# Conditioning's sums in 32 by 32 squares on VectorE, and an embedding gate that begins with the first tile of tokens

## What is computed

```
# first block, from its second half on
hn = rms_norm(h, g_ffn_pre)
f_gate, f_up = split(hn @ w_ffn_in)              # 1024 -> 2 x 2816
f = (silu(f_gate) * f_up) @ w_ffn_out
h = h + rms_norm(f, g_ffn_post)
h = h + sigmoid(h @ w_ple_gate) * (p @ w_ple)    # the embedding's gate

# second block
cond = silu(c)                                   # 1024 values
mod = cond @ w_ada + b_ada                       # 1024 -> 6144
shift_mix, scale_mix, gate_mix, shift_ffn, scale_ffn, gate_ffn = split(mod)
h = rmsnorm(x, g_mix) * (1 + scale_mix) + shift_mix
qkv = h @ w_in                                   # then two kinds of attention,
                                                 # w_out, routing to 2 of 32 experts
```

## Time and profile before

| | us |
|---|---|
| median of 3 runs | 1155.83 |
| lowest and highest | 1154.67, 1155.89 |
| the profiled execution | 1153.45 |
| its span, first to last instruction | 1151.6 |
| TensorE busy | 1045.0 (91%) |
| VectorE busy | 492.2 (43%) |
| ScalarE busy | 377.3 (33%) |
| GpSimd busy | 493.2 (43%) |

### The profile page before, as it was taken

The page is one execution under the profiler, slowest core; times in us unless marked ns, Lnnn a source line. Parts: engine busy times, 40 slices in busy tenths (PEclk is TensorE's granted clock), DMA queues, the critical chain, the costliest instruction groups (busy, mean ns, idle before and its releaser), DMA issues.

```text
span 1151.6 us, 19857 instructions
## 1 busy us (share of the span) xinstructions
PE 1045.0 (91%) x8566; PEld 804.7 (70%) x8566; DVE 492.2 (43%) x886; ACT 377.3 (33%) x539; POOL 493.2 (43%) x209
## 2 busy tenths in 40 slices
PE   7999999998999999999999999898877788878676
PEld 6988999998799999888898895344433343424232
DVE  2999948467355465032245643222222121212112
ACT  6454544543654444444495432000000000000001
POOL 6895889875787888946465410000000000000000
PEclk9999999999999999999899999999999898989998
DMA  9554454356579989754233679999999999999994
GB/s 367 197 185 146 174 186 181 146 229 232 225 278 337 340 324 341 262 173 164 108 147 125 261 289 420 420 420 419 420 421 420 421 420 419 420 422 420 419 421 164
DMA packets 48330, 342.16 MB, mean 297 GB/s; under 512 B 5361, under 2 KB 5745, under 8 KB 7410
## 3 DMA queue, kind: packets, MB, share of 16 engines
q1 hardware_dynamic: 46944, 337.56, 74.3%
q10 hardware_dynamic: 1298, 3.32, 0.8%
HBM read 339.81 MB, written 1.05 MB: 296 GB/s over the span
## 4 chain that ended last, share of the span: by engine, by line
PE 60%; DMA 22%; DVE 11%; ACT 2%; SPq 2%; issue 1%; POOL 1%; DVEq 0%; ACTq 0%
DMA ring<-in_gu 17%; PE ps L469 14%; PE ps L471 14%; PE ps L470 14%; PE ps L1037 5%; DVE ps L1645 5%; DMA ar<-in_gu 5%; PE ps L1084 4%; PE ps L1073 2%; PE ps L1017 2%; SPq L2286 2%; PE ps L711 1%; POOL spl L2220 1%; DMA raw<-in_stream 1%; PE ps L462 1%
## 5 line engine op out<-in xcount | busy, mean ns | idle before, releaser
L2220 POOL TENSOR_TENSOR spl<-raw,sph 128x1024 fp32r<-128x1024 f32 x204 | 492.7, 2453 | 177.3 <-ACT sph L1139 177.2
L1139 ACT ACTIVATE sph<-raw 128x1024 fp32r<-128x1024 f32 x204 | 206.3, 1055 | 143.9 <-DMA raw<-in_stream 85.5
L469 PE MATMUL ps<-xbh,sph 128*128 128x256 f32 x608 | 173.5, 285 | 4.2 <-DVE xbl L1625 2.5
L470 PE MATMUL ps<-xbl,sph 128*128 128x256 f32 x608 | 172.7, 284 | 0.0
L471 PE MATMUL ps<-xbh,spl 128*128 128x256 f32 x608 | 172.7, 284 | 0.0
L469 PE MATMUL ps<-xah,sph 128*128 128x256 f32 x576 | 165.0, 286 | 1.1 <-DVE xal L1615 0.8
L470 PE MATMUL ps<-xal,sph 128*128 128x256 f32 x576 | 163.0, 283 | 0.0
L471 PE MATMUL ps<-xah,spl 128*128 128x256 f32 x576 | 162.9, 283 | 0.0
L2170 DVE TENSOR_TENSOR ar<-ar,ps 64x256 f32<-64x256 f32 x32 | 13.5, 423 | 275.4 <-ACT ar L1561 275.4
L1561 ACT ACTIVATE ar<-ps 64x256 f32<-64x256 f32 x32 | 12.1, 378 | 350.1 <-PE ps L1037 350.1
L1084 PE MATMUL ps<-ar,ar 128*128 128x512 f32 x256 | 125.7, 636 | 0.0
(11 more groups left out here) (292 smaller groups left out, 1337.3 us busy)
## 6 DMA issues: line engine op xcount, KB each, us to landing
raw<-in_stream SPq DMA_DIRECT2D x127, 1024.0 KB, 4.9
ring<-in_gu SPq DMA_DIRECT2D x116, 1024.0 KB, 27.0
ring<-in_dn SPq DMA_DIRECT2D x57, 1024.0 KB, 27.2
slotx<-in_gu SPq DMA_DIRECT2D x6, 1024.0 KB, 28.3
ar<-in_gu SPq DMA_DIRECT2D x6, 1024.0 KB, 26.3
ar<-in_dn SPq DMA_DIRECT2D x4, 1024.0 KB, 26.8
slotx<-in_dn SPq DMA_DIRECT2D x3, 1024.0 KB, 28.1
X<-in_x SPq DMA_DIRECT2D x2, 512.0 KB, 4.4
```

What stands on the lines that cost most here:

```text
L469: e.matmul(o, sh, mh, start=start, stop=False)
L470: e.matmul(o, sh, ml, start=False, stop=False)
L1139: e.activation(u.half(SPH[u.n % NSP], h), u.half(RAW[u.slot], h), ACTF.Copy).then_inc(w.up(hi_ok), 1)
L2220: e.tensor_tensor(u.half(SPLO[u.n % NSP], h), u.half(RAW[u.slot], h), u.half(SPH[u.n % NSP], h), ALU.subtract).then_inc(w.up(lo_ok), 1)
```

## The change

Five things change.

- Blocks of `w_ada` (the ten for the first 5120 columns): the last step stays in PSUM, and two instructions of VectorE follow every second unit. A transpose of each square of 32 by 32 brings 512 partial sums for each partition to `ADT`; a sum over 32 neighbours leaves 16 values in `ADS`. The sum over the partitions is then done but for its four groups of 32.
- `FOLD`, made once from the identity, adds these four groups up: four products of 32 by 40 on TensorE (L725 of the changed kernel) give all 40 columns of `MC` at once, between first-tile and second-tile work of the gate. The two `columns` are gone, and VectorE adds the bias for all 40 at once, ahead of the first gated quarter.
- X is turned a tile at a time, into two banks with one tile each: tile 0 ahead of w_ffn_out's last unit for tile 1, tile 1 behind the fold. ScalarE and VectorE copy tile by tile as well.
- The gate goes: unit 0 and 1 for tile 0; fold; tile 1 turned; unit 2 for tile 0; units 0, 1, 2 for tile 1; unit 3 for tile 0; unit 3 for tile 1. The quarters end in the order 0, 2, 1, 3 (`PARTS`), and sigmoids and gated sums follow it. On ScalarE the splits of later units now stand between the sigmoids in another way.
- Counts of semaphores follow. A slot of `RAW` is still free after the unit's four steps, not after the pair.

```diff
+        ADT = ADA[:, 4096:4608].rearrange("p (m c) -> p m c", m=16)
+        ADS = ADA[:, 4608:4768]
+        FOLD = ADA[:, 4768:4800]
...
             held.discard(ab)
-            free[ab] = [(ada_ok, 16)]
+            free[ab] = [(ada_ok, 20)]
             bb = token_major("w_out", XA, landed("merge", 1))
...
             for tt in ((0, 1), (0,), (1,)):
                 for c in range(8) if len(tt) == 2 else range(8, 11):
+                    if c == 10 and tt == (1,):
+                        turn_x2(0)
...
+                for s in range(4):
+                    mm = e.matmul(ps[b][32 * s:32 * s + 32, 0:40], FOLD, ADS.rearrange("p (j s) -> p s j", s=4)[:, s, :],
+                                  start=True, stop=True)
...
-            columns(0, 24)
+            part(0, 0, False, False)
+            part(1, 0, False, False)
+            held.clear()
+            held.update(gb)
+            turn_at[0] = bb[2]
+            columns()
             turn_x2(1)
-            bb = token_major("ple_gate", XB, landed("x2", 2))
+            part(2, 0, True, False)
+            part(0, 1, False, True)
+            part(1, 1, False, True)
+            part(2, 1, True, True)
+            part(3, 0, True, False)
+            part(3, 1, True, True)
...
             turn_old(0)
-            columns(24, 40)
...
                 if tt == 0:
                     take(wide_at[9])
                     take(wide_at[10])
+                    x2_high(0)
-            for n in range(4):
-                w.wait_ge(xt_mm, n + 1)
-                high(("x2", n), XB, 2 * n, None)
+            take(first["ple_gate"])
+            x2_high(1)
...
-            take(first["ple_gate"])
+            gate(0)
             take(first["ple_gate"] + 1)
-            gate(0)
-            gate(1)
             gate(2)
             take(first["ple_gate"] + 2)
+            gate(1)
             take(first["ple_gate"] + 3)
             gate(3)
...
+                if m % 2 and j < 10:
+                    own()
+                    e.transpose(ADT.rearrange("p m c -> p (m c)"), acc).then_inc(w.up(ada_ok), 1)
+                    own()
+                    e.tensor_reduce(ADS[:, 16 * j:16 * j + 16], ADT, AX, ALU.add).then_inc(w.up(ada_ok), 1)
...
+            e.tensor_reduce(FOLD, ident.rearrange("p (q r) -> p r q", q=4), AX, ALU.add).then_inc(w.up(az_ok), 1)
...
-                            w.wait_ge(ada_ok, 4 * ada_at.index(v - NRAW) + 4)
+                            w.wait_ge(ada_ok, ada_used[ada_at.index(v - NRAW)])
```

More of the change, by code:

```diff
@@ L682, in tensor, with turn_x2 @@
             held.update(bb)
+            def turn_x2(tt):
+                w.wait_ge(x_ok, X2 + 4 * tt + 4)
+                for half in range(2):
+                    b = bank(("x2", tt, half))
+                    claim(b)
+                    for k in range(4):
+                        o = (4 * half + k) * 128
+                        mm = e.transpose(ps[b][:, 128 * k:128 * k + 128], X[:, tt, o:o + 128], ident)
+                    mm.then_inc(w.up(xt_mm), 1)
+                    free[b] = [(act_lo, part_at["x2"] + 2 * tt + half + 1)]
             for tt in ((0, 1), (0,), (1,)):
                 for c in range(8) if len(tt) == 2 else range(8, 11):
+                    if c == 10 and tt == (1,):
+                        turn_x2(0)
                     w.wait_ge(ffm_ok, behind(c))
@@ L692, in tensor @@
             free[ab] = [(ada_ok, N_ADA)]
-            xb = [bank(("x2", n)) for n in range(4)]
-            def turn_x2(tt):
-                w.wait_ge(x_ok, X2 + 4 * tt + 4)
-                for k in range(8):
-                    o = (k % 2) * 256 + tt * 128
-                    claim(xb[k // 2])
-                    mm = e.transpose(ps[xb[k // 2]][:, o:o + 128], X[:, tt, k * 128:k * 128 + 128], ident)
-                    if tt and k % 2:
-                        mm.then_inc(w.up(xt_mm), 1)
@@ L713, in columns @@
                 mm.then_inc(w.up(mc_mm), 1)
-                free[b] = [(mc_ok, 2 if j0 else 1)]
-            turn_x2(0)
+                free[b] = [(mc_ok, 1)]
+            xb0 = [bank_of["x2", 0, half] for half in range(2)]
             held.clear()
-            held.update(xb)
+            held.update(xb0 + bb[2:])
             turn_at[0] = bb[0]
-            columns(0, 24)
-            turn_x2(1)
-            held.clear()
-            for n in range(4):
-                free[xb[n]] = [(act_lo, part_at["x2"] + 2 * n + 2)]
@@ L725, in tensor, with part @@
-            turn_at[0] = bb[0]
-            bb = token_major("ple_gate", XB, landed("x2", 2))
+            gb = [bank(("ple_gate", q)) for q in range(4)]
+            outs = [[ps[gb[2 * tt + j]][:, :] for tt in range(2)] for j in range(2)]
+            def part(n, tt, begun, done):
+                if n % 2 == 0:
+                    claim(gb[2 * tt + n // 2])
+                ready = None if begun else lambda k: (act_lo, part_at["x2"] + 2 * tt + k // 4 + 1)
+                tm_part("ple_gate", n, outs[n // 2], XB, ready, (tt,), done)
@@ L1878, in vector, with x2_low @@
                 m += 1
+            def x2_low(tt):
+                for half in range(2):
+                    c = slice(128 * tt, 128 * tt + 128)
+                    w.wait_ge(act_hi, part_at["x2"] + 2 * tt + half + 1)
+                    own()
+                    e.tensor_tensor(XB[1][:, 4 * half:4 * half + 4, c], k4(ps[bank_of["x2", tt, half]]),
+                                    XB[0][:, 4 * half:4 * half + 4, c], ALU.subtract).then_inc(w.up(act_lo), 1)
             w.wait_ge(d_gfp, 16)
```

62 lines of the change are left out of this document (33 added, 29 removed).

## The result

| | before | after |
|---|---|---|
| median, us (lowest, highest; 4 runs each) | 1155.66 (1154.67, 1155.89) | 1141.7 (1140.1, 1143.05) |
| span of the profiled execution | 1151.6 | 1138.2 |

The ratio is 0.9885, with a 95% interval of 0.9869 to 0.9902. In two later comparisons it was 0.9889 both times (0.9871 to 0.9906, 0.9868 to 0.991). The direction was right. The two profiled spans differ by 13.4.

A forecast was written before the change was run, and what follows sets the result against it. Bound: the expert-weight stream fills the DMA engines from 680 us but can start earlier, so time saved on the chain before 640 us counts. 8.05 + 2.17 - 1.5 = 8.7 us off 1155.83 gives 1147.1; range 1145.0 to 1150.8.

The forecast's parts named there:

- sum A: From the end of w_ffn_out to the gate's end on TensorE: 32.55 us becomes 24.5, a gain of 8.05.
- sum B: From the gate's end to the third norm's reciprocal: 5.90 us becomes 3.73, a gain of 2.17.
- sum C: VectorE's added transpose and sum: conv_out's second pair, ahead of the gated sum, is uncovered and costs 1.5 us.
- pairs under w_ffn_in: Eight transpose-and-sum pairs on VectorE while TensorE is busy: cost nothing, with 3.3 us to spare.
- covers of 0.8 to 1.1 us: Time to spare for the gate's operands, such as GpSimd's split halves; if lost, 2.35 us at most.
- Rival 1: VectorE's pair waits for GpSimd: slower beyond 4.7 us a pair, up to 1163.9 (chance 0.04); pair of 2.5 to 4.7, 0.05.
- Rival 2: The gate does not run dense, for a late split half or a clock fall: 1148.8 to 1151.1 us, chance 0.15.
- Turning X alone: Part of rival 2, in the gate: X's turns by themselves make the clock fall, chance 0.07 of the 0.15.
- the 1148.8: Time in us if the clock falls in the gate, as it would if transposes do not count as busy.

The follow-up runs named there:

- before_again: The kernel before, run once more with nothing edited: one run of 1155.13 us, span 1153.3.
- gate_only: The gate's new order alone, with the 24 and 16 column products kept and no transposes: 1154.77 us, 0.9993 of the kernel before.
- sums_only: The sums in squares and the fold alone, in the gate's order of before: 1148.52 us, 0.9951 of the kernel before.
- before_pad28: The kernel before plus 28 one-column products that nothing reads, two in each of fourteen experts: 1151.74 us, 0.9979 of the kernel before.

## Why the prediction was wrong, point by point

| step | predicted | measured in the traces |
|---|---|---|
| sum A, to the gate's end | -8.05 | -8.6 |
| sum B, to the reciprocal | -2.17 | -2.2 |
| sum C, the pair in conv_out | +1.5 | +1.5 in the first profile, +1.05 in the mean |
| pairs under w_ffn_in | 0 | 0 |
| clock behind the gate | 0 | -1.05 in the first profile, -0.7 in the mean |
| TensorE's branch at the end | not looked at | -2.3 in the first profile, -2.75 in the mean |
| start of the kernel | 0 | -0.5 in the first profile, +0.4 in the mean |

The sums are cut at the fourth sigmoid: from w_ffn_in's first product it begins 219.50 us later in the kernel before and 210.91 in the changed one, and from it to the diagonal's product it is 6.51 and 4.35. The means are of two profiles of before and three of after; with -10.7 for A and B, and -0.1 in the experts, they add up to -12.8, which is the difference of the mean spans, 1152.4 and 1139.6, and fits the three ratios, 0.9885 to 0.9889 (0.9888 of the 1155.2 that 49 runs of before have as their median is 12.9 less). The first comparison's 14.0 has a microsecond of luck in it.

**Sum A** had the mechanism and its places right. No operand came late, and the covers of 0.8 to 1.1 us held: GpSimd's splits never made TensorE wait. Its fold was mis-sized. I took it at 0.9 from one-column products of 128 rows, eight records one after the other; it took 0.26, near the end that I had called "next to nothing", since four of its records start within 20 ns. That is 0.6, and the whole of what sum A was off by (0.5).

**Sum B and sum C** came out as worked out, 2.2 and 1.5. (The mean has 1.05 for the pair since one of its two profiles of before is before_again, whose conv_out took 46.92. Its clock fell at 285.1 for 6.8 us; gate_only has such a fall at 286.3 and only 46.31, so that this is the reason isn't shown. The five profiles without pairs have 46.28 in the mean, the six with one pair on the path 47.51.) Transpose and sum took 716 and 686 ns, inside the bounds. Rival 1 is gone: neither instruction took longer beside a busy GpSimd, and at 1.46 us the pair is far from 4.7. The Trainium skill's warning of tensor_reduce (VectorE: DVE Perf Modes, Rules for kernel authors) holds in its rate: 686 ns for 512 elements and 1220 for 1024 differ by 534 ns for 512 elements, about one a nanosecond. It was no reason against the change, because the instruction took work from TensorE, and at nine of ten places VectorE had the time to spare.

**Rival 2**, a fall of the clock in the gate, had 0.15. It didn't happen in any of the eight runs with both halves. It did in both runs with one half, so it was the right thing to fear. But the prediction misread how it comes about. It has the clock fall "in the first hole after 5.9 us of one-column products". In the kernel before it fell at 512.8, with 1.4 us of these products still to come, while TensorE was busy without a gap (windows, PEclk third from the end):

```profile
511.00:514.00 3.00, 3.00 (x24) 3.00 (x25) 0.14 (x1) 0.00 (x0) 0.39 (x1) 0.80 0.47 131
```

The records before the fall start 0.112 us apart and those behind it 0.214, so that 0.124 is a mean over both levels. In gate_only it fell in the same products, at 518.4, with dense ones right ahead of them. So a hole was not needed for it. In the eight profiles with neither these products nor a hole it didn't fall in the gate; in sums_only there was a hole, of 2.52 us. Turning X alone didn't let the clock fall here: granted 1.00 from 510 to 530. The Trainium skill (TensorE: Matmul & The Clock Gate, Part 4: PE-mode transpose) says that transposes don't count as busy; eight of them between dense products changed nothing here, and the 1148.8 that a fall would have given wasn't seen.

**The step that failed** is the total's silence on everything behind the gate. I read the stretch from 640 us on as a stream that only shifts. It does: the experts took 432.3 and 432.1. But the kernel doesn't end with it: of the last 3.4 us of the kernel before, 3.06 were a single branch of TensorE. This is the largest term that the prediction had at nothing, 2.3 us in the first profile and 2.75 of the 4.1 us by which the mean was off. The prediction listed what the change removes by the time of each instruction, and never asked what 144 fewer records do to the code itself. It read no view of the last 5 us, where one row (3060 ns beside 72, 50 and 45 on the other engines) would have shown a stall of the right size. To tell from it that this change would take it away, one would have had to work out where the code ends in a block; with that in doubt, it was a rival of about 1144.

**The clock behind the gate** is the smaller miss. In the six runs with at most one half of the change, the way to the experts took 149.3 each time; in the eight with both it was 148.1 to 148.4 four times and 149.3 to 149.5 four times. Whether the second fall comes in a given execution isn't decided by anything that I found, so it stays open. Four and four against none in six could still be chance.

## What to carry to other kernels

Read the last microseconds of the trace as closely as the stage of the change: a branch there waited 3 us for its instructions, and whether it did hung on the length of the code, so that an edit elsewhere can bring or take 2.7 us: 36 idle products brought it, and 28 took it away. When a change has two parts, ask what each removed piece of work was covering: column products on TensorE hid a wait for VectorE, and without the new order more than half of what they had cost came back, as idle time (2.5 us) and as products at the lower clock. Price a step by where it stands; the same 1.5 us of VectorE cost 1.2 to 1.5 at one place, nothing at nine others, and nothing once moved behind the work that ScalarE waited for.

## What the runs showed of the hardware

- The branch at the end took TensorE 0.37 to 0.47 us where no instruction packet came in it, and 3.06 to 3.89 where one did; the last stage goes with it (21.02 to 21.04 us against 23.37 to 24.18). A long one ended 1.4 to 1.5 us after its packet was through.
- Eight records of 32 by 40 products went by in 0.26 us, about 33 ns each. The four products write 32 partitions of the bank each, and their records start 7 ns apart, four at a time. Records of a one-column product with 128 rows start 112 ns apart at the upper clock and 214 at the lower one.
- The clock fell while TensorE was busy with such one-column products, 4.6 us into them in before and 2.6 in gate_only; it stayed up through the new gate, with its 0.3 us of fold and 0.9 of turn.
- A VectorE transpose in 32 by 32 squares of 128 by 512 floats from PSUM to SBUF took 716 ns, hardly more than a copy of that size (692); the sum of 512 floats into 16 took 686.
- Most stages repeat to 0.1 us from run to run and chip to chip. What spreads the profiles by some 3 us is when the clock falls: a fall at 98 us in five of fourteen, worth 1.5 us, a second one behind the gate, which goes with 1.1 us more in that stage, and a longer one in the last expert (6.8 us for 3.4, in four profiles), which goes with 1.3 more. In before_pad28 the fall at the gate's beginning was half as long as in before, and the gate's column is 1.7 us less.
